# Running sums by token inside the expert loop, in place of a last stage that gathers the experts' rows

## The chip, the core and the metric

The kernel runs on one NeuronCore of a Trainium2 chip. The metric is the time of one execution in microseconds (us) on the device. Three executions of the kernel before took 1806.34, 1813.04 and 1813.47 us; the median is 1813.04 us. Engines: PE is TensorE (PEld its weight loads), ACT is ScalarE, DVE is VectorE, POOL is GpSimd, SP is SyncE, which here only issues transfers. Each engine runs its own instructions in order; a wait on a semaphore holds up everything behind it on that engine.

## The reference, cut to what matters

One layer of a streaming encoder for 1088 tokens (1024 of a prompt, 64 of a sample) of width 1024. The change touches its end:

```
  h = x + w_out( sum_b sigmoid(gate_b) * (o_b @ w_branch[b]) )
  h = h + HierMoE(rmsnorm(h))   (top-1 of 4 groups, then top-2 of 8 SwiGLU experts)
  y = rmsnorm_final(h)

def expert_block(args):
    xblk, e = args
    return (jax.nn.silu(xblk @ wg[e]) * (xblk @ wu[e])) @ wd[e]

def rmsnorm(x, g):
    x32 = x.astype(jnp.float32)
    y = x32 * lax.rsqrt(jnp.mean(x32 * x32, axis=-1, keepdims=True) + EPS)
    return (y * g.astype(jnp.float32)).astype(x.dtype)
```

Each token goes to 2 of the 32 experts, so there are 2176 pairs of token and expert, 68 for an expert in the mean. Each expert has three weight matrices of 2 MB. All is in float32.

## The kernel before

The program is a row of stages. The last one, which the change is in, is one block: gates and branches, the output projection (which leaves the rows h in SBUF as `mixT`, and `hlast` for the last 64 tokens), routing, 32 experts, and a tail.

**Routing** (VectorE `choose` and `take`, TensorE `count` and `enlist`) gives each pair a place: up to 128 tokens in the list of their expert. The list (`toks`) says which rows of the normalised h, kept in device memory as `ffn_rows` (`htd`), expert n needs. GpSimd fetches them by an indirect DMA into `xe` (L2021), two experts ahead at most.

**An expert** n on TensorE: `turn_x` transposes the fetched rows, `up(n,"g")` and `up(n,"u")` are the gate and up products, `turn_h` transposes the hidden rows, `down(n)` is the down product. In the order of the program `down(n-1)` comes after `up(n,"u")` and `turn_x(n+1)`, so one turn of the loop holds 72 matmuls of 512 columns. Each product is made in three passes from halves in a rounded format: of each half matrix (128x2048, 1 MB, six for an expert) ScalarE writes the high part `hig` (`split_high`, L2434), VectorE the low part `low`<-`raw`,`hig` (`split_low`, L2732). There are 8 buffers of raw and low halves and 6 of high ones. SP issues each 1 MB load as its buffer comes free.

**ScalarE's turn n** is written out by hand: two splits, `silu(n)` (L2496), `h_high(n-1)` (L2500), two splits, `x_high(n+1)` (L2489), two splits, `out(n-1)` (L2507), which copies the finished rows of expert n-1 from PSUM to `ye`, and the issue of their store to `expert_rows` (`ysd`, L2510). VectorE's turn has its six splits and `h_low`, `multiply`, `x_low`. In turns 8, 11 and 14 VectorE does, one a turn, `overflow`, `order` and `slots`, which work out the weights of the pairs and their places (`sidx`); `slots` ends with the semaphore `found`.

**The tail** begins when the experts' rows are in device memory. For nine tiles of tokens GpSimd gathers each token's two expert rows (`ya` L2033 and L2058, `yb` L2051); four tiles are summed on TensorE by diagonal matrices (L2318, L2327, L2334), five on VectorE (L2924, L2930). ScalarE squares and takes the root (L2577 to L2581), VectorE scales (L2937), SP stores.

A list of more than 128 tokens goes on in a loop of its own (`further`), which waits for `found` and does nothing for these inputs.

## Time and profile before

The profiled execution took 1812.19 us, of which the span from its first to its last instruction is 1810.5 us.

| engine | busy us | share of the span |
|---|---|---|
| PE | 1760.3 | 97% |
| DVE | 1047.7 | 58% |
| ACT | 860.7 | 48% |
| POOL | 118.8 | 7% |

The experts run from about 1192 us to 1763 us, a third of the span, with PE busy throughout; the tail is the rest. The 16 DMA engines are busy for all of the expert stage too. Shares over the whole span say little here: in the expert stage DVE is busy for nine tenths and ACT for eight tenths of the time, POOL for less than one.

### The profile page before, as it was taken

The page shows a single profiled execution, that of the slowest core. Times are in us where ns is not written, and L with a number is a line of the kernel's source. Part 1 is how long each engine was busy: PE and PEld are TensorE (multiplying, and loading weights), DVE is VectorE, ACT ScalarE, POOL GpSimd, SP SyncE. Part 2 cuts the span into 40 slices and gives each one's busy share as a digit, 9 for nine tenths or more (in the row PEclk, how much of TensorE's full clock was granted, in tenths as well). Part 3 has the DMA queues.
Part 4 walks back from the last instruction along what each step waited for, and adds up shares of the span by engine and source line. Part 5 has one row for each costly group of instructions (what it writes and reads, how often), then busy time and mean ns, then how long its engine had stood idle before and what let it go on. Part 6 is the DMA issues. An engine that isn't in the chain of part 4 may idle for free.

```text
span 1810.5 us, 25543 instructions
## 1 busy us (share of the span) xinstructions
PE 1760.3 (97%) x10346; PEld 1562.7 (86%) x10346; DVE 1047.7 (58%) x1303; ACT 860.7 (48%) x1093; POOL 118.8 (7%) x139
## 2 busy tenths in 40 slices
PE   8999999999999999999999999989999999999995
PEld 7888888988898899999999988878888888888872
DVE  5347775433445431223243255678989998898965
ACT  4225554331543331211122223268887878788863
POOL 0010000000000020000000000010000000000024
PEclk9999999999999999999999999989999999999997
DMA  5241111112122132222221232189999999999987
GB/s 189 85 120 30 31 32 37 35 32 60 35 64 83 41 98 64 88 63 83 70 99 47 76 146 71 65 331 403 419 408 417 414 413 415 414 415 415 415 290 262
DMA packets 140762, 329.42 MB, mean 182 GB/s; under 512 B 15978, under 2 KB 92646, under 8 KB 115941
## 3 DMA queue, kind: packets, MB, share of 16 engines
q1 hardware_dynamic: 123764, 272.25, 40.7%
q0 software_dynamic: 12128, 38.74, 5.9%
q10 hardware_dynamic: 4752, 16.78, 2.3%
q8 instruction: 84, 1.38, 0.3%
q14 instruction: 34, 0.28, 0.0%
HBM read 290.09 MB, written 39.87 MB: 182 GB/s over the span
## 4 chain that ended last, share of the span: by engine, by line
PE 61%; DVE 1%; DMA 1%; DVEq 0%; issue 0%; ACT 0%; ACTq 0%; POOLq 0%
PE banks L72 7%; PE banks L70 7%; PE banks L71 7%; PE banks L2233 6%; PE banks L2235 6%; PE banks L2234 6%; PE banks L2261 3%; PE banks L2259 3%; PE banks L2260 3%; PE banks L2112 2%; PE banks L2114 2%; PE banks L2113 2%; PE banks L2219 2%; PE banks L2243 1%; PE banks L2142 1%; DMA yb<-expert_rows,sidx 1%
## 5 line engine op out<-in xcount | busy, mean ns | idle before, releaser
L2732 DVE TENSOR_TENSOR low<-raw,hig 128x2048 fp32r<-128x2048 f32 x192 | 431.4, 2285 | 58.0 <-ACT hig L2434 55.6
L2434 ACT ACTIVATE hig<-raw 128x2048 fp32r<-128x2048 f32 x192 | 359.3, 1916 | 20.8 <-ACT ye L2507 14.5
L2233 PE MATMUL banks<-hig,xel 128*128 128x512 f32 x512 | 203.1, 397 | 0.2 <-DVE xel L2804 0.2
L2235 PE MATMUL banks<-hig,xeh 128*128 128x512 f32 x512 | 200.2, 391 | 0.0
L2234 PE MATMUL banks<-low,xeh 128*128 128x512 f32 x512 | 199.8, 390 | 0.0
L70 PE MATMUL banks<-xhi,glo 128*128 128x384 f32 (+1 forms) x552 | 180.0, 326 | 1.9 <-PEq L65 1.9
L72 PE MATMUL banks<-xhi,ghi 128*128 128x384 f32 (+1 forms) x552 | 180.0, 326 | 0.0
L71 PE MATMUL banks<-xlo,ghi 128*128 128x384 f32 (+1 forms) x552 | 179.9, 326 | 0.0
L70 PE MATMUL gproj<-xhi,glo 128*128 128x384 f32 (+1 forms) x384 | 130.1, 339 | 0.0
L72 PE MATMUL gproj<-xhi,ghi 128*128 128x384 f32 (+1 forms) x384 | 125.4, 326 | 0.0
L71 PE MATMUL gproj<-xlo,ghi 128*128 128x384 f32 (+1 forms) x384 | 125.2, 326 | 0.0
L2235 PEld LDWEIGHTS banks<-hig,xeh 128*128 128x128 f32 x512 | 96.4, 188 | 20.7
L2233 PEld LDWEIGHTS banks<-hig,xel 128*128 128x128 f32 x512 | 96.8, 189 | 19.6 <-DVE xel L2804 0.6
L2234 PEld LDWEIGHTS banks<-low,xeh 128*128 128x128 f32 x512 | 96.5, 189 | 19.0
L2625 DVE TENSOR_TENSOR tm<-sg,banks 128x384 f32<-128x384 f32 (+1 forms) x42 | 22.3, 532 | 152.2 <-PE banks L72 152.2
L836 DVE TENSOR_TENSOR_SCAN sfx<-sfx,over 128x896 f32<-128x896 f32 (+4 forms) x64 | 85.6, 1389 | 34.7 <-ACT sfx L672 34.7
L70 PEld LDWEIGHTS banks<-xhi,glo 128*128 128x128 f32 x552 | 103.6, 188 | 2.0 <-issue 2.0
L72 PEld LDWEIGHTS banks<-xhi,ghi 128*128 128x128 f32 x552 | 103.6, 188 | 0.0
L71 PEld LDWEIGHTS banks<-xlo,ghi 128*128 128x128 f32 x552 | 103.6, 188 | 0.0
L2259 PE MATMUL banks<-hig,htl 128*128 128x512 f32 x256 | 102.6, 401 | 0.0
L2261 PE MATMUL banks<-hig,hth 128*128 128x512 f32 x256 | 100.0, 391 | 0.0
L2260 PE MATMUL banks<-low,hth 128*128 128x512 f32 x256 | 99.9, 390 | 0.0
(484 smaller groups left out, 3510.9 us busy)
## 6 DMA issues: line engine op xcount, KB each, us to landing
raw<-in_w_e_gate_dram SPq DMA_DIRECT2D x64, 1024.0 KB, 8.1
raw<-in_w_e_up_dram SPq DMA_DIRECT2D x64, 1024.0 KB, 8.2
raw<-in_w_e_down_dram SPq DMA_DIRECT2D x64, 1024.0 KB, 7.5
graw<-in_w_in_dram SPq DMA_DIRECT2D x39, 512.0 KB, 3.8
expert_rows<-ye ACTq DMA_DIRECT2D x31, 512.0 KB, 8.3
xt<-in_x_prompt_dram SPq DMA_DIRECT2D x16, 512.0 KB, 3.6
expert_rows<-nil POOLq DMA_DIRECT2D x16, 512.0 KB, 4.0
braw<-in_w_branch_dram SPq DMA_DIRECT2D x24, 256.0 KB, 3.0
```

The costliest lines, as they stand in the source:

```text
L70: nc.tensor.matmul(out, wl, xh, start=(opens and i == 0), stop=False)
L71: nc.tensor.matmul(out, wh, xl, start=False, stop=False)
L72: last = nc.tensor.matmul(out, wh, xh, start=False, stop=(closes and i == len(parts) - 1))
L836: nc.vector.tensor_tensor_scan(v, v, cover, 1.0, ALU.mult, ALU.max).then_inc(scanned, 1)
L2233: nc.tensor.matmul(bank[:, :], xel[n % 2][:, kk, :], wh[:, k, :], start=(kk == 0), stop=False)
L2234: nc.tensor.matmul(bank[:, :], xeh[n % 2][:, kk, :], wl[:, k, :], start=False, stop=False)
L2235: last = nc.tensor.matmul(bank[:, :], xeh[n % 2][:, kk, :], wh[:, k, :], start=False, stop=(kk == KC - 1))
L2259: nc.tensor.matmul(bank[:, :], htl[n % 2][:, kk, :], wh[:, k, cols], start=(kk == 0), stop=False)
L2260: nc.tensor.matmul(bank[:, :], hth[n % 2][:, kk, :], wl[:, k, cols], start=False, stop=False)
L2261: last = nc.tensor.matmul(bank[:, :], hth[n % 2][:, kk, :], wh[:, k, cols], start=False, stop=(kk == 3))
L2434: nc.scalar.activation(hig[q % HI][:, :], raw[q % RAW][:, :], ACT.Copy).then_inc(high, 1)
L2732: nc.vector.tensor_tensor(low[q % RAW][:, :], raw[q % RAW][:, :], hig[q % HI][:, :].bitcast(F32), ALU.subtract).then_inc(lowed, 1)
```

## The change

The kernel after has no tail that gathers. A second array in device memory, `sum_rows` (`acd`), starts as a copy of h, a row for each token. Every expert adds its rows, already multiplied by the pair's weight, to the running sums. The lower-numbered expert of a token writes the sum back (`low_rows`); the higher-numbered one has the complete row of the token, so the final norm of that row is taken there and the row goes to the output (`out_rows`). Rows that a transfer shall leave out have an index beyond its bound.

- **GpSimd** for expert c: `sum_rows` (an indirect DMA that reads the token's sums and adds them into `ye`), two `out_rows` for expert c-2 (prompt and sample), `root_of(c-1)`: one multiplication of 128x1024 by the norm weight and 13 operations on one column with a drain behind each but the first (a root by Newton's steps), then the wait for `hr_in` and `low_rows`. `sum_rows` waits for `low_out`: the write-back of expert c-1 has to be in memory.
- **ScalarE**: `square(n-2)` after `silu(n)`, waiting for `hr_in`, that is for `sum_rows(n-2)`; and before `out(n-1)` a multiplication of a 128x1024 row block by the roots (waiting for `rooted_row`). The store is no longer issued here. For the first three experts GpSimd multiplies by the weight, since the weights by place are not there yet.
- **VectorE**: `overflow` and `order` at the end of turn 0, `slots` at the end of turn 1. `slots` now makes records of 8 words (`smeta`: token, weight, three destinations).
- **GpSimd before its loop**: 9 more stores (`sum_rows` from `mixT`), and after `found` 18 indirect scatters of the records by place, a wait for them, and two loads of the records in the experts' order (`meta`, 32 bytes for each place).
- The last two experts' sums are added on VectorE (`hr`), and the last three experts' rows are scaled there.

The diff, cut to its core:

```diff
+        def low_rows(pool, src, which, signal):
+            pool.indirect_dma_start(acd, bass.IndirectOffsetOnAxis(ap=which[:, 2:3], axis=0), src[:, :], None,
+                                    bounds_check=T - 1, oob_is_err=False).then_inc(signal, 16)
+
+        def out_rows(pool, src, which, signal):
+            pool.indirect_dma_start(yp, bass.IndirectOffsetOnAxis(ap=which[:, 3:4], axis=0), src[:, :], None,
+                                    bounds_check=FULL * P - 1, oob_is_err=False).then_inc(signal, 16)
+            pool.indirect_dma_start(ysm, bass.IndirectOffsetOnAxis(ap=which[:, 4:5], axis=0), src[:, :], None,
+                                    bounds_check=T - FULL * P - 1, oob_is_err=False).then_inc(signal, 16)
...
+            nc.gpsimd.tensor_scalar(tokg[:, :], tokf[:, :], float(-T), None, ALU.add)
+            nc.gpsimd.memset(smp[:, 0:FULL], float(FAR))
+            nc.gpsimd.tensor_scalar(smp[:, FULL:NT], tokf[:, FULL:NT], float(-FULL * P), None, ALU.add)
...
             for t in range(NT):
                 r = rows_of(t)
                 pool.wait_ge(ndone, t + 1)
                 pool.dma_start(htd[t * P:t * P + r, :], nrow[t % 2][0:r, :]).then_inc(kept[t % 2], 16)
+                pool.dma_start(wide(acd[t * P:t * P + r, :]), hrow(t, r)).then_inc(hkept, 16)
...
-            for n in range(NE):
+            def x_rows(n):
                 if n >= 2:
                     pool.wait_ge(xturned, 2 * n - 2)
+                places = toks2[:, n:n + 1] if n < 2 else toks[:, n:n + 1]
+                pool.indirect_dma_start(xe[n % 2][:, :], None, htd, bass.IndirectOffsetOnAxis(ap=places, axis=0),
+                                        bounds_check=T - 1, oob_is_err=False).then_inc(fetched[n % 2], 16)
+
+            def sum_rows(n, dst, compute):
+                pool.wait_ge(low_out, 16 * n)
+                pool.indirect_dma_start(dst[:, :], None, acd, bass.IndirectOffsetOnAxis(ap=toks[:, n:n + 1], axis=0),
+                                        bounds_check=T - 1, oob_is_err=False, compute_op=compute).then_inc(hr_in, 16)
+
+            def root_of(c):
+                pool.wait_ge(squared, c + 1)
+                ms, x, y, u = stat[:, c:c + 1], root[:, 0:1], root[:, 1:2], root[:, 2:3]
+                if c >= 2:
+                    pool.wait_ge(y_out[c % 2], 32 * (c // 2))
+                nc.gpsimd.tensor_tensor(yo[c % 2][:, :], ye[c % YE][:, :], gf[:, :], ALU.mult).then_inc(gained, 1)
+                nc.gpsimd.tensor_scalar(x, ms, EPS, None, ALU.add)
+                pool.drain()
+                nc.gpsimd.tensor_copy(u, x.bitcast(I32))
+                pool.drain()
+                nc.gpsimd.tensor_scalar(u, u, -0.5, 1597463007.0, ALU.mult, ALU.add)
+                pool.drain()
+                nc.gpsimd.tensor_copy(y.bitcast(I32), u)
+                pool.drain()
+                for _ in range(3):
+                    nc.gpsimd.tensor_scalar(u, y, y, x, ALU.mult, ALU.mult)
+                    pool.drain()
+                    nc.gpsimd.tensor_scalar(u, u, -0.5, 1.5, ALU.mult, ALU.add)
+                    pool.drain()
+                    nc.gpsimd.tensor_scalar(y, y, u, None, ALU.mult)
+                    pool.drain()
+                pool.wait_ge(gained, c + 1)
+                pool.sem_inc(rooted_row, 1)
+
+            def finish(c):
+                pool.wait_ge(scaled, c + 1)
+                out_rows(pool, yo[c % 2], meta[:, c, :], y_out[c % 2])
...
+            x_rows(2)
+            x_rows(3)
+            pool.wait_ge(filled, 16)
             pool.wait_ge(found, 1)
+            for t in range(NT):
+                for k in range(2):
+                    pool.indirect_dma_start(slot_meta, bass.IndirectOffsetOnAxis(ap=sidx[k][0:r, t:t + 1], axis=0),
+                                            smeta[0:r, t, k, :], None).then_inc(meta_out, 16)
+            pool.wait_ge(meta_out, 16 * 2 * NT)
...
+            for c in range(NE - 2):
+                if c + 4 < NE:
+                    x_rows(c + 4)
+                if c == 0:
+                    pool.wait_ge(meta_in0, 16)
+                if c == 4:
+                    pool.wait_ge(meta_in1, 16)
+                pool.wait_ge(emptied, c + 1)
+                if c < YE:
+                    nc.gpsimd.tensor_scalar(ye[c][:, :], ye[c][:, :], share(c), None, ALU.mult).then_inc(shared, 1)
+                    pool.wait_ge(shared, c + 1)
+                sum_rows(c, ye[c % YE], ALU.add)
+                if c >= 2:
+                    finish(c - 2)
+                if c:
+                    root_of(c - 1)
+                pool.wait_ge(hr_in, 16 * c + 16)
+                low_rows(pool, ye[c % YE], meta[:, c, :], low_out)
...
             def out(n):
-                if n >= 2:
-                    act.wait_ge(stored[n % 2], 16 * (n // 2))
+                if n >= YE:
+                    act.wait_ge(gained, n - YE + 1)
+                    act.wait_ge(low_out, 16 * (n - YE + 1))
                 act.wait_ge(used, place["d", n, 1] + 1)
+                if n == YE:
+                    act.wait_ge(meta_in0, 16)
+                if n == YE + 1:
+                    act.wait_ge(meta_in1, 16)
                 for half in range(2):
-                    last = nc.scalar.activation(ye[n % 2][:, half * 512:half * 512 + 512], [Z0, Z1][half][:, :], ACT.Copy)
+                    last = nc.scalar.activation(ye[n % YE][:, half * 512:half * 512 + 512], [Z0, Z1][half][:, :], ACT.Copy,
+                                                scale=share(n) if n >= YE else 1.0)
                 last.then_inc(emptied, 1)
+            def square(c):
+                if c < NE - 2:
+                    act.wait_ge(hr_in, 16 * c + 16)
+                else:
+                    act.wait_ge(joined, 1)
+                nc.scalar.activation(junk[:, :], ye[c % YE][:, :], ACT.Square, scale=D ** -0.5,
+                                     accum_out=stat[:, c:c + 1]).then_inc(squared, 1)
...
                     split_high(q0 + 4)
                     split_high(q0 + 5)
                     silu(n)
+                if 2 <= n < NE:
+                    square(n - 2)
...
                     split_high(q0 + 9)
                     if n == NE - 1:
                         h_high(n)
+                    if n >= 3:
+                        act.wait_ge(rooted_row, n - 2)
+                        nc.scalar.activation(yo[(n - 3) % 2][:, :], yo[(n - 3) % 2][:, :], ACT.Copy, scale=root[:, 1:2]).then_inc(scaled, 1)
                     out(n - 1)
...
+                nc.vector.memset(smf[:, :, :, :], 0.0)
...
+                both = lambda t: t[:, :].unsqueeze(2).to_broadcast([P, NT, 2])
+                nc.vector.tensor_copy(smf[:, :, :, 0], both(tokf))
+                nc.vector.tensor_tensor(smf[:, :, :, 2], pair[:, :, :], both(tokf), ALU.add)
+                ve.drain()
+                nc.vector.tensor_tensor(smf[:, :, :, 3], isov[:, :, :], both(tokf), ALU.add)
+                nc.vector.tensor_tensor(smf[:, :, :, 4], isov[:, :, :], both(smp), ALU.add)
...
+                nc.vector.tensor_copy(smeta[:, :, :, 1].bitcast(F32), wts[:, :, :]).then_inc(found, 1)
...
-                if n in (8, 11, 14):
-                    (overflow, order, slots)[(n - 8) // 3]()
+                if n == 0:
+                    overflow()
+                    ve.drain()
+                    order()
+                    ve.drain()
+                if n == 1:
+                    slots()
```

ScalarE in two turns of the expert loop. Before, from the end of one turn to the end of the next (`hig` is a split, `gl` the silu, `hth` h_high, `xeh` x_high, `ye` the rows of the finished expert):

```order
L2507 ACTIVATE ye_7119<-banks 128x512 x2
L2510 DMA expert_rows<-ye_7119 128x1024
L2434 ACTIVATE hig_7102<-raw_7084 128x2048
L2434 ACTIVATE hig_7103<-raw_7085 128x2048
L2496 ACTIVATE gl_7121<-banks 128x512
L2500 ACTIVATE hth_7112<-banks 128x512
L2434 ACTIVATE hig_7104<-raw_7086 128x2048
L2434 ACTIVATE hig_7105<-raw_7087 128x2048
L2489 ACTIVATE xeh_7108<-banks 128x512 x2
L2434 ACTIVATE hig_7100<-raw_7088 128x2048
L2434 ACTIVATE hig_7101<-raw_7089 128x2048
```

After, the same stretch up to the multiplication that now stands ahead of `ye`:

```order
L2525 ACTIVATE ye_7120<-banks,meta_7128 128x512 x2
L2448 ACTIVATE hig_7104<-raw_7086 128x2048
L2448 ACTIVATE hig_7105<-raw_7087 128x2048
L2509 ACTIVATE gl_7134<-banks 128x512
L2534 ACTIVATE junk_7127,stat_58<-ye_7120 128x1024
L2513 ACTIVATE hth_7114<-banks 128x512
L2448 ACTIVATE hig_7106<-raw_7088 128x2048
L2448 ACTIVATE hig_7107<-raw_7089 128x2048
L2502 ACTIVATE xeh_7110<-banks 128x512 x2
L2448 ACTIVATE hig_7102<-raw_7090 128x2048
L2448 ACTIVATE hig_7103<-raw_7091 128x2048
L2562 ACTIVATE yo_7124<-yo_7124,root_7071 128x1024
```

`junk,stat<-ye` is the square, which stands directly behind the silu and ahead of h_high and four splits; `yo<-yo,root` is the multiplication by the roots, with the next `ye` behind it; the store is gone.

GpSimd in the expert loop. Before, the last two of its 32 fetches, which stand one behind the other, and the first gathers of the tail:

```order
L2021 DMA xe_7106<-ffn_rows,toks_7116 128x1024
L2021 DMA xe_7107<-ffn_rows,toks_7116 128x1024
L2033 DMA ya_7130<-expert_rows,sidx_7041 128x1024
L2033 DMA ya_7138<-expert_rows,sidx_7041 64x1024
L2033 DMA ya_7131<-expert_rows,sidx_7041 128x1024
```

After, the last third of one expert's work and the first half of the next's (the column work on `root` stands 13 times for each expert):

```order
L2027 TENSOR_SCALAR root_7071<-root_7071 128x1
L2029 TENSOR_SCALAR root_7071<-root_7071 128x1
L2031 TENSOR_SCALAR root_7071<-root_7071 128x1
L1904 DMA sum_rows<-ye_7122,meta_7128 1088x1024
L2004 DMA xe_7109<-ffn_rows,toks_7118 128x1024
L2009 DMA ye_7120<-sum_rows,toks_7118 128x1024
L1908 DMA out_dram<-yo_7125,meta_7128 1024x1024
L1910 DMA out_dram<-yo_7125,meta_7128 64x1024
L2017 TENSOR_TENSOR yo_7124<-ye_7122,gf_7126 128x1024
L2018 TENSOR_SCALAR root_7071<-stat_58 128x1
L2020 CAST root_7071<-root_7071 128x1
L2022 TENSOR_SCALAR root_7071<-root_7071 128x1
```

The fetch of `xe` was all there was for an expert. Now the add from `sum_rows`, two stores to the output, the multiplication by `gf` and the chain on `root` stand between two write-backs to `sum_rows`.

## Rows read from the trace of the kernel before

**Rows 1.** Window in the expert stage: us, busy (count) by engine, PEclk, DMA share, GB/s.
```profile
1350.00:1400.00 50.00, 50.00 (x239) 41.97 (x238) 45.37 (x41) 40.85 (x36) 4.39 (x3) 1.00 1.01 413
```

**Rows 2.** Timeline of ACT, one turn: start, us, instruction, idle before it and its releaser.
```profile
1396.87 1.09 ACT L2489 ACTIVATE xeh<-banks 128x512 fp32r<-128x512 f32 x2 [1.29 <-PE banks L2219]
1397.84 3.72 ACT L2434 ACTIVATE hig<-raw 128x2048 fp32r<-128x2048 f32 x2
1402.85 1.09 ACT L2507 ACTIVATE ye<-banks 128x512 f32<-128x512 f32 x2 [1.28 <-PE banks L2261]
...
1404.40 3.72 ACT L2434 ACTIVATE hig<-raw 128x2048 fp32r<-128x2048 f32 x2 [0.47 <-ACT ye L2507]
...
1408.23 0.60 ACT L2496 ACTIVATE gl<-banks 128x512 f32<-128x512 f32 x1
1408.73 0.59 ACT L2500 ACTIVATE hth<-banks 128x512 fp32r<-128x512 f32 x1
...
1414.63 1.09 ACT L2489 ACTIVATE xeh<-banks 128x512 fp32r<-128x512 f32 x2 [1.70 <-PE banks L2219]
```

**Rows 3.** DMA issues, the end of a row being the median us to landing.
```profile
ffn_rows<-nrow POOLq DMA_DIRECT2D x1, 256.0 KB, 7.3
wr<-in_w_fine_dram POOLq DMA_DIRECT2D x4, 32.0 KB, 4.0
```

**Rows 4.** Tile xe: its 32 fetches, us from issue to landing.
```profile
DMA to landing us min/median/max: 4.4/8.6/9.8
```

**Rows 5.** Timeline, DVE's splits beside POOL's indirect DMAs, experts and last expert.
```profile
1411.79 4.49 DVE L2732 TENSOR_TENSOR low<-raw,hig 128x2048 fp32r<-128x2048 f32 x2
1415.30 1.80 POOL L2021 DMA_INDIRECT xe<-ffn_rows,toks  x1 [16.38 <-PE banks L2219]
1752.17 4.49 DVE L2732 TENSOR_TENSOR low<-raw,hig 128x2048 fp32r<-128x2048 f32 x2
1752.47 2.87 POOL L2033 DMA_INDIRECT ya<-expert_rows,sidx  x1 [0.30 <-issue]
```

**Rows 6.** Timeline about 130 us, and the group of DVE's line 789 (ns min/median/max).
```profile
129.85 1.68 POOL L361 TENSOR_TENSOR vn<-vsh,vn 64x512 f32<-64x512 f32 x1 [6.14 <-DMA vsh<-in_cache_sb_v_dram]
130.78 2.54 DVE L789 TENSOR_TENSOR vn<-vsh,vn 128x512 f32<-128x512 f32 x1
131.50 1.26 POOL L340 TENSOR_TENSOR cvs<-cvsh,cvs 128x512 f32<-128x512 f32 x1
...
L789 DVE TENSOR_TENSOR vn<-vsh,vn x8: 681/686/2535, 124.9 to 143.2; 128x512 f32<-128x512 f32 x8
```

**Rows 7.** POOL timeline, two casts with drains between; and a group of the tail.
```profile
3.36 0.59 POOL L345 CAST qbh<-nbias 64x64 fp32r<-64x64 f32 x2 [1.04 <-DVE identb L859]
...
L2051 POOL DMA_INDIRECT yb<-expert_rows,sidx x9 | 9.0, 997 | 4.2 <-issue 2.4 <-DMA expert_rows<-ye 1.8
```

**Rows 8.** ACT and DVE in turns 1 and 2; windows about `overflow`, `order` and `slots`.
```profile
1222.27 4.50 DVE L2732 TENSOR_TENSOR low<-raw,hig 128x2048 fp32r<-128x2048 f32 x2
1231.19 0.59 ACT L2500 ACTIVATE hth<-banks 128x512 fp32r<-128x512 f32 x1
...
1351.00:1353.00 2.00, 2.00 (x11) 1.65 (x10) 1.58 (x12) 1.85 (x2) 0.00 (x0) 1.00 0.97 365
1404.20:1406.90 2.70, 2.70 (x14) 2.23 (x13) 2.40 (x12) 2.50 (x2) 0.00 (x0) 1.00 1.03 413
1457.50:1461.70 4.20, 4.20 (x23) 3.54 (x21) 3.68 (x23) 3.93 (x3) 0.00 (x0) 1.00 0.99 394
```

**Rows 9.** The end: chain of waits (first two rows), then timeline of ACT and DVE.
```profile
1757.51 1.09 ACT ye L2507 x2
1765.83 9.93 DMA yb<-expert_rows,sidx
...
1797.18 1.04 ACT L2577 ACTIVATE junk<-ya 128x1024 f32<-128x1024 f32 x1
...
1798.51 1.28 DVE L2930 SCALAR_TENSOR_TENSOR ya<-ya,wts,yb 128x1024 f32<-128x1024 f32 x1
```

More of the change, by code:

```diff
@@ L2037, in body @@
+            c = NE - 2
+            sum_rows(c, hr, ALU.bypass)
+            finish(c - 2)
+            pool.wait_ge(joined, 1)
+            low_rows(pool, ye[c % YE], meta[:, c, :], low_out)
+            sum_rows(c + 1, hr, ALU.bypass)
+            for i in range(3):
+                c = NE - 3 + i
+                pool.wait_ge(last_scaled, i + 1)
+                out_rows(pool, last_yo[i], meta[:, c, :], y_out[c % 2])
             def body(b, e):
```

379 lines of the change are left out of this document (133 added, 246 removed).

## The prediction

> **What bounds the kernel now.** I read the windows first. In the expert stage PE has no gap: 50.00 of 50.00 us at a granted clock of 1.00, while DVE works 45.37, ACT 40.85 and POOL 4.39 us, and the DMA engines are busy throughout [rows 1]. The timeline of ACT shows the rhythm: x_high at 1396.87 and again at 1414.63, so an expert costs 17.76 us [rows 2]. Between, ACT idles only 3.4 us: 1.28 and 1.70 us waiting for PE, 0.47 us before it issues a store [rows 2]. So this stage goes at PE's pace, with ACT and DVE close behind. After the last matmul comes a tail: from the start of the copy of expert 30's rows (1757.51) to the end of the span (1810.5) it is 53.0 us, or 51.9 us from that copy's end, nearly all chain [rows 9]. The chain there shows one gather awaited for 9.93 us. The change trades this tail for work in a stage where ACT has 3.4 us an expert to spare, DVE some 1.6 us, and POOL, by its busy time, 16 us.
>
> The sum is made against the profiled execution: 1812.2 us, of which 1810.5 us are its span; that is 0.8 us under the median of 1813.04 us.
>
> **The tail: what goes and what comes.** From the end of the copy of expert 30's rows it now takes: an addition on DVE at 1.3 us; `low_rows(30)`; `sum_rows(31)`; two halves on DVE for expert 31, 1.3 us together; the second half of the square, 0.8 us with reading its sum; logarithm and exponential with drains, 0.7 us (estimate); scaling on DVE, 1.3 us; two stores, the second issued 1.3 us behind the first, and landed. The durations are those of L2930 (1.28) and half of L2577 (1.04) with its read-out [rows 9]; the issue is 1.0 us with 0.3 us behind it [rows 7]. Each round trip is priced at 4.4 us, the quickest fetch there was, since no weights are loaded then [rows 4]; at 8.6 us each it would be 12.6 us more. Sum: 1.3 + 4.4 + 4.4 + 1.3 + 0.8 + 0.7 + 1.3 + 1.3 + 4.4 = 19.9, with hops 20.9 us. Against 51.9 us that is **31 us gained**, between 18 and 34.
>
> **The start of the experts.** ScalarE's turn 2 has `square(0)` behind its silu, which waits for the sums of expert 0, and those need the records. Before, turn 2's h_high, right behind the silu, stood at 1231.19 [rows 8]. Now VectorE ends turn 1's splits at 1226.8; `overflow` (2.0 us), `order` (2.7 us) and `slots` (4.2 us, now about 5 as it has some more small steps) are put before `found` [rows 8]: 1226.8 + 2.0 + 2.7 + 5 = 1236.5. Then 18 scatters on POOL at 1.3 us [rows 7]: 1259.9. The last has to land, some 3.4 us after its issue (4.4 less 1.0) [rows 4, 7]; the first load of records takes 4 us, as one of 1024 pieces of 32 bytes does [rows 3]: 1267.3. A multiplication by the weight on POOL, 2 us (L340 takes 1.26 for two inputs of 512 columns [rows 6]), then `sum_rows(0)` at 7.3 us (priced below) and about 4 us because 3584 pieces of 32 bytes are ahead of it in its queue: 1280.6. So ACT stands from 1231 to about 1281. All that is behind it stands too: h_high(1), without which `down(1)` can't start, the splits for expert 3, x_high. PE runs out of work within 8 us. Nothing gives this back later, since PE has no slack: **50 us lost**; at best 35 (records in at once, fetch 4.4 us), at worst 85, if each of the 224 small pieces an engine has is served in turn with a 4 KB piece of weights. The nine extra stores of h during routing are beside idle DMA engines; I take 1 us for the last one, which is ahead of the first fetch, and count it in the hops.
>
> **Each expert, first by the round trip.** The add for expert c can be issued when `out(c)` is done. ACT then does two splits (3.7 us) and the silu, and comes to `square(c)` about 4.9 us after the end of `out(c)`: 1403.94 to 1408.83 [rows 2]. The transfer moves 68 rows or 272 KB in the mean. The nearest row is the 256 KB one that ran beside the first weight loads: 7.3 us; ends 4.4 and 9.8 us [rows 3, 4]. So ACT waits here in every turn. From the landing to the end of `out(c+1)` ACT has: square 1.2, h_high 0.5, two splits 3.6, x_high 1.0, two splits 3.6, the new multiplication 1.0, out 1.1 = 12.0 us [rows 2, 9]. The circle is 12.0 + 0.2 + 7.3 = 19.5 us against 17.76: 1.7 us more for each expert. It is free from 5.5 us down.
>
> **Then by POOL.** There is a second circle: `sum_rows(c)` must wait for the write-back of c-1, which POOL issues behind all its other work. From the issue of the add: 1.3; two stores 2.6; the multiplication of 1024 columns 2.5 (twice 1.26 [rows 6]); 13 column operations at 0.36 us, the spacing of two small casts with a drain between them (0.59 less 0.23 for one) [rows 7], 4.7; sum 11.1 us. `low_rows` then takes 6.5 us from issue to landing (136 KB: between 4.0 for 32 KB and 7.3 for 256 KB [rows 3]). That is 17.6 us, which would just fit into 17.76.
>
> But POOL does not run beside DVE's splits as if alone. At 1415.30 an indirect DMA was issued while the second of two splits ran until 1416.28; it took 1.80 us instead of 1.0 and ended 0.8 us after the split. At 1752.47 one ended 0.9 us after the first split of its pair (1754.42), 2.87 us in all [rows 5]. It goes the other way too: a VectorE subtraction that takes 686 ns took 2535 while POOL had two subtractions of its own until 132.76, and ended 0.56 us after them [rows 6]. Whoever is second waits for the other's instruction to end. The two-input splits, 2.24 us each and six for an expert, are 13.5 us of each turn. A chain of 13 dependent column operations that meets a pair of splits gets one operation through at each end of a split, in place of six.
>
> With these I lay out one turn from the issue of the add, with the landing at 7.3: splits of the down half run until about 3.6, those of the gate half from 11 to 15.5, those of the up half from 17.5. The two stores lose some 2.2 us to the first pair, the column chain, which would end at 13.3, loses 3.7 us to the second and ends at 17. The write-back lands at 17 + 6.5 = 23.5 us. **23.5 us for an expert**, 5.75 more than now. The low end is the round-trip circle at 4.4 us, which costs nothing; the high end is 27 us (write 8 us, four more waits of a split), 9.3 more. I take 5.75, since the lock is seen in rows on both sides. 28 turns (experts 1 to 29) see it: **161 us lost**.
>
> The Trainium skill says the same as a rule (SBUF — State Buffer, § Who interferes with whom): a VectorE instruction with two SBUF inputs contends with a GpSimd instruction that reads SBUF, as an exclusive lock held for the whole instruction. It would hold for the small column operations as well, which no row here shows; the trace agrees for indirect DMAs and for subtractions [rows 5, 6]. Without it the sum would be that of the round-trip circle.
>
> DVE gets less time too: POOL's multiplication by `gf` can block a split for 2.5 us, and DVE has 1.6 us to spare; in a turn of 23.5 us that is hidden.
>
> Sum: 1812.2 - 31 + 50 + 161 = **1992 us**.
>
> **Rivals.**
> *A, round trips only.* The small column operations slip by the splits, and ACT's wait for the add sets the pace at 19.5 us: 1812.2 - 31 + 50 + 28 x 1.7 = 1879 us. For it: only indirect DMAs and wide subtractions are seen to wait. Against it: column operations read SBUF through the same port as those.
> *B, latency hides.* With 68 rows in place of 128 the add lands within 5.5 us and POOL's chain fits. Then only start and tail count: 1812.2 - 31 + 50 = 1831 us. For it: fewer rows, and the fastest fetch at 4.4 us. Against it: the 256 KB transfer beside the weights took 7.3 us, and the median fetch took 8.6 [rows 3, 4]. The Trainium skill (DMA: Bandwidth & Descriptors, § Anatomy of one DMA — SWDGE path) puts a transfer at about 2.0 us plus its bytes at 436 GB/s, an estimate of 2.6 us for 272 KB, by which B would hold; for the 512 KB fetches it says 3.2 us and the trace 8.6, so I weigh it low.
> *C, the records come in time.* If ACT does not stand in turn 2 for longer than 31 us, and the turns stay at 17.76, the tail decides and the kernel is faster: at a stand of 15 us, 1812.2 - 31 + 15 = 1796 us. Against it: the 18 scatters alone are 23.4 us behind `found`, itself 5 us after ACT has arrived.
> *D, worse than laid out.* Turns at 27 us or over, or the small pieces at their dear price: 1812.2 - 31 + 50 + 28 x 9.3 = 2092 us and more.
>
> **How the numbers follow.** Forecast (turns of 21.5 to 26 us) 0.52, own range 1930 to 2070; A 0.25; B 0.08; C 0.04; D 0.11. The range for 8 in 10 leaves out C, most of B and most of D: 1845 to 2100 us. A change under 0.5% (9 us) can't be told from none. Faster by more holds only in C: 0.04. Within it: 0.02, from B with a shorter stand. Slower: 0.94.
>
> **What would show it.** In the changed profile: ACT idle for 40 to 60 us before `junk`<-`ye` in turn 2, PE idle with it; 18 `slot_meta`<-`smeta` scatters just before. Then x_high every 23 to 24 us (19.5 for A, 17.8 for B), POOL busy or held for most of a turn, and its `root` operations in clusters with gaps that end where a split of DVE ends. The add <-`sum_rows` landing at 6 to 8 us. The wait ahead of the add is for `low_out`, not for ACT's `ye`; if it is for ACT's `ye` in every turn, A holds. A span that ends about 21 us after the last expert but one is copied out shows the tail. The forecast fails if the column operations run at even spacing through the splits, or if the add lands within 5.5 us.

## The result

The changed kernel takes 2203.11 us (median of 4 executions, 2201.55 to 2207.49) where the kernel before takes 1813.16 us: a ratio of 1.2174, 95% interval 1.2154 to 1.2194. The profiled execution took 2201.55 us, its span 2199.9 us. The direction was forecast, the size was not: 390 us more in place of 180, outside the range of 1845 to 2100 us.

The span grew by 389.4 us. Three marks of the two timelines cut it up:

| stretch | before | after | difference |
|---|---|---|---|
| start of h_high(1), ScalarE's turn 2 | 1231.19 [rows 8] | 1272.00 | +40.8 |
| from there to the end of the copy of expert 30's rows | 527.4 us | 899.5 us | +372.1 |
| from there to the end of the span | 51.95 us | 28.47 us | -23.5 |

So nearly all of it is in the turns of the expert loop (the stretch holds 29 of them).

### The profile after

The window that answers to [rows 1], the same columns:

```profile
1400.00:1500.00 100.00, 69.49 (x289) 56.89 (x289) 54.24 (x36) 51.99 (x48) 62.85 (x62) 0.85 0.67 237
```

PE, without a gap before, is busy for 69 of 100 us. No engine is near its limit and the DMA engines are a third idle: this is a loop of waits, not a lack of throughput. The granted clock of PE is down to 0.85, a mean over stretches at the full clock (2.4 GHz) and at the lower one (1.2 GHz), but PE is waiting in any case.

One turn on GpSimd (start, length, engine, line, what; in brackets the idle time before):

```profile
1692.08 1.60 POOL L2009 DMA_INDIRECT ye<-sum_rows,toks  x1 [5.41 <-DMA sum_rows<-ye,meta]
1693.98 1.04 POOL L1908 DMA_INDIRECT out_dram<-yo,meta  x1 [0.30 <-issue]
1695.32 0.98 POOL L1910 DMA_INDIRECT out_dram<-yo,meta  x1 [0.30 <-issue]
1696.32 2.36 POOL L2017 TENSOR_TENSOR yo<-ye,gf 128x1024 f32<-128x1024 f32 x1
1698.76 0.24 POOL L2018 TENSOR_SCALAR root<-stat 128x1 f32<-128x1 f32 x1
1701.34 0.18 POOL L2020 CAST root<-root 128x1 f32<-128x1 int32 x1 [2.34 <-issue]
...
1703.23 2.41 POOL L2031 TENSOR_SCALAR root<-root 128x1 f32<-128x1 f32 x1 [0.17 <-issue]
1705.83 2.15 POOL L2027 TENSOR_SCALAR root<-root 128x1 f32<-128x1 f32 x1 [0.18 <-issue]
...
1709.74 2.06 POOL L2029 TENSOR_SCALAR root<-root 128x1 f32<-128x1 f32 x1 [0.16 <-issue]
1711.97 2.14 POOL L2031 TENSOR_SCALAR root<-root 128x1 f32<-128x1 f32 x1 [0.17 <-issue]
1715.07 1.06 POOL L1904 DMA_INDIRECT sum_rows<-ye,meta  x1 [0.96 <-issue]
1716.43 1.05 POOL L2004 DMA_INDIRECT xe<-ffn_rows,toks  x1 [0.30 <-issue]
1724.42 1.60 POOL L2009 DMA_INDIRECT ye<-sum_rows,toks  x1 [6.95 <-DMA sum_rows<-ye,meta]
```

The next add waits for the write-back (6.95 us), so GpSimd's circle sets the turn. (A drain stands behind each of the 13 column operations, the first too.) Two things in it are not as forecast. Ahead of the first cast, behind the first drain, there are 2.34 us that nothing named accounts for. And four operations on a single column take 2.1 to 2.4 us where their neighbours take 0.2 to 0.3. ScalarE and VectorE in that turn:

```profile
1699.80 1.06 ACT L2534 ACTIVATE junk<-ye 128x1024 f32<-128x1024 f32 x1 [9.97 <-DMA ye<-sum_rows,toks]
...
1701.34 3.70 ACT L2448 ACTIVATE hig<-raw 128x2048 fp32r<-128x2048 f32 x2
...
1714.25 1.15 ACT L2562 ACTIVATE yo<-yo,root 128x1024 f32<-128x1024 f32 x1 [4.64 <-POOLq L2034]
```

```profile
1701.47 0.69 DVE L2818 TENSOR_TENSOR htl<-banks,hth 128x512 fp32r<-128x512 f32 x1 [9.40 <-ACT hth L2513]
1703.27 4.49 DVE L2739 TENSOR_TENSOR low<-raw,hig 128x2048 fp32r<-128x2048 f32 x2 [1.11 <-ACT hig L2448]
...
1709.47 4.48 DVE L2739 TENSOR_TENSOR low<-raw,hig 128x2048 fp32r<-128x2048 f32 x2
```

The long column operations are those beside VectorE's splits. In the turn ahead of this one they are twice as long, one operation for both splits of a pair (GpSimd, then VectorE):

```profile
1672.60 4.57 POOL L2027 TENSOR_SCALAR root<-root 128x1 f32<-128x1 f32 x1 [0.18 <-issue]
...
1672.54 4.50 DVE L2739 TENSOR_TENSOR low<-raw,hig 128x2048 fp32r<-128x2048 f32 x2 [1.11 <-ACT hig L2448]
```

Between 1350 and 2100 us, 59 of the 312 operations on `root` are long, and each of the 59 ends 0.05 to 0.22 us after the end of a split: 34 take 2.0 to 2.5 us, 25 take 4.3 to 4.6 us. VectorE had stood idle for 9.40 us before, while ScalarE waited for the add; the landing of the add lets ScalarE, VectorE and GpSimd's chain go all at once. Averaged over 27 turns of the loop (worked out from the timelines):

| us from the issue of the add | forecast | measured |
|---|---|---|
| add landed, the square starts | 7.3 | 8.8 |
| second column operation starts | 8.6 | 10.1 |
| chain ends | 17.0 | 21.7 |
| write-back issued | 17.0 | 22.7 |
| next add issued (the turn) | 23.5 | 30.6 |

At the end, the last adds, writes and scaling run as described, in 28.5 us. The first row is expert 30's sum on VectorE, 6.2 us after the copy of its rows; the others are the last on GpSimd:

```profile
2177.64 1.23 DVE L2928 TENSOR_TENSOR ye<-ye,hr 128x1024 f32<-128x1024 f32 x1 [10.04 <-DMA hr<-sum_rows,toks]
...
2183.11 1.04 POOL L2009 DMA_INDIRECT hr<-sum_rows,toks  x1 [2.21 <-DMA sum_rows<-ye,meta]
...
2188.34 0.96 POOL L1910 DMA_INDIRECT out_dram<-yo,meta  x1 [0.30 <-issue]
2192.36 0.96 POOL L1908 DMA_INDIRECT out_dram<-last_yo,meta  x1 [3.06 <-DVE last_yo L2934]
2193.62 0.96 POOL L1910 DMA_INDIRECT out_dram<-last_yo,meta  x1 [0.30 <-issue]
```

### The profile page after: what moved, and what is told of

Read it like the earlier page. It is cut to its first block and busy times, and to the rows that moved or that the text cites. A ratio compares the mean times of both kernels' runs of the same rounds, so it can differ in the third digit from the quotient of the medians.

```text
span 2199.9 us, 26544 instructions
## 1 busy us (share of the span) xinstructions
PE 1806.6 (82%) x10298; PEld 1600.5 (73%) x10298; DVE 1033.9 (47%) x1280; ACT 907.0 (41%) x1154; POOL 641.1 (29%) x666
## 5 line engine op out<-in xcount | busy, mean ns | idle before, releaser
L2302 PE MATMUL banks<-hig,htl 128*128 128x512 f32 x256 | 132.2, 516 | 343.4 <-DVE htl L2818 343.4
L2302 PEld LDWEIGHTS banks<-hig,htl 128*128 128x128 f32 x256 | 64.6, 252 | 364.3 <-DVE htl L2818 349.4
L2534 ACT ACTIVATE junk<-ye 128x1024 f32<-128x1024 f32 x31 | 32.7, 1056 | 373.3 <-DMA ye<-sum_rows,toks 367.8
L2818 DVE TENSOR_TENSOR htl<-banks,hth 128x512 fp32r<-128x512 f32 x32 | 22.1, 691 | 343.9 <-ACT hth L2513 343.7
L2303 PE MATMUL banks<-low,hth 128*128 128x512 f32 x256 | 125.0, 488 | 0.0
L2304 PE MATMUL banks<-hig,hth 128*128 128x512 f32 x256 | 122.0, 477 | 0.0
L2031 POOL TENSOR_SCALAR root<-root 128x1 f32<-128x1 f32 x87 | 107.1, 1231 | 14.8 <-issue 14.8
L2278 PEld LDWEIGHTS banks<-hig,xeh 128*128 128x128 f32 x512 | 96.2, 188 | 20.6
```

What stands on the lines that cost most here:

```text
L2031: nc.gpsimd.tensor_scalar(y, y, u, None, ALU.mult)
L2278: last = nc.tensor.matmul(bank[:, :], xeh[n % 2][:, kk, :], wh[:, k, :], start=False, stop=(kk == KC - 1))
L2302: nc.tensor.matmul(bank[:, :], htl[n % 2][:, kk, :], wh[:, k, cols], start=(kk == 0), stop=False)
L2303: nc.tensor.matmul(bank[:, :], hth[n % 2][:, kk, :], wl[:, k, cols], start=False, stop=False)
L2304: last = nc.tensor.matmul(bank[:, :], hth[n % 2][:, kk, :], wh[:, k, cols], start=False, stop=(kk == 3))
```

## The experiments

The theory after the first look: (a) a drain on GpSimd also waits for every transfer that GpSimd has under way, so the chain can't start before the add and the stores have landed; (b) that start coincides with VectorE's splits, which hold up the chain. The rivals: the forecast's A (ScalarE's wait for the add sets the turn), and that the slow column operations or the gap have some other cause. All kernels start from the changed one (2203 us). The turn, and its parts, are means in us over 27 or 28 turns. "Add landed" counts from the add's issue; "chain" is the time from the second column operation's start to the last one's end.

| run | us | turn | add landed | chain | what differs |
|---|---|---|---|---|---|
| changed kernel | 2203 | 30.6 | 8.8 | 11.6 | |
| e1 | 2025 | 24.0 | 11.2 | 4.0 | semaphores for drains |
| e2 | 2089 | 26.8 | 11.4 | 2.5 | no Newton steps (leaves out part of the root) |
| e3 | 2200 | 30.7 | 10.0 | 10.5 | write-back ahead of the chain |
| e4 | 2192 | 30.1 | 10.2 | 10.1 | e1 and e3 |
| e5 | 2089 | 26.8 | 7.3 | 5.9 | square at the end of the turn |
| e6 | 2183 | 30.2 | 10.1 | 10.0 | splits of VectorE halved |
| e7 | 2063 | 25.9 | 7.6 | 5.9 | e1 and e5 |
| e8 | 2149 | 28.4 | 15.2 | 4.0 | e1 and e6 |
| e9 | 1972 | 22.7 | 9.8 | - | root on VectorE, two Newton steps |
| e10 | 1934 | 21.6 | 11.6 | - | e9, square late, write-back first |
| e11 | 2215 | 31.0 | 11.1 | 9.0 | stores behind the write-back |
| e12 | 1907 | 20.6 | 10.5 | - | e10, fetch behind the add |

### e1: semaphores in place of drains

```
+            def link(inst):
+                inst.then_inc(linked, 1)
+                links[0] += 1
+                pool.wait_ge(linked, links[0])
...
-                nc.gpsimd.tensor_copy(u, x.bitcast(I32))
-                pool.drain()
+                link(nc.gpsimd.tensor_copy(u, x.bitcast(I32)))
```

> GpSimd's 13 column operations are tied together by a semaphore each in place of a drain; nothing else. The changed kernel has a mean turn of 30.6 us. Theory (the turn is one chain on GpSimd: the add lands 8.8 us after its issue, a drain that waits for every transfer GpSimd has under way ends 1.3 us later, 12 column operations held up by VectorE's splits take 11.6, the write-back is issued 1.0 later and lands after 8.0): without drains the chain starts some 7 us after the add's issue in place of 10.1, so 3 us less for each expert, 2203 - 28 x 3 = about 2120 us, and the idle time ahead of the first cast falls from 3.1 us a turn to 0.2. Rival (that idle time is VectorE's lock or a fixed cost of the chain): 2203 us, within 10.

Measured: 2024.62 us, 178 us less, twice what was expected (some 83). One turn on GpSimd, first and last rows of the chain:

```profile
1706.62 2.83 POOL L2009 DMA_INDIRECT ye<-sum_rows,toks  x1 [6.11 <-ACT ye L2525]
...
1713.25 2.40 POOL L2024 TENSOR_TENSOR yo<-ye,gf 128x1024 f32<-128x1024 f32 x1
1715.75 0.24 POOL L2025 TENSOR_SCALAR root<-stat 128x1 f32<-128x1 f32 x1
1716.05 0.18 POOL L2026 CAST root<-root 128x1 f32<-128x1 int32 x1
...
1719.79 0.28 POOL L2032 TENSOR_SCALAR root<-root 128x1 f32<-128x1 f32 x1
1720.99 2.78 POOL L1904 DMA_INDIRECT sum_rows<-ye,meta  x1 [0.92 <-POOL root L2032]
```

The gap ahead of the cast is gone, and every column operation is short. VectorE's timeline says why:

```profile
1703.50 8.89 DVE L2739 TENSOR_TENSOR low<-raw,hig 128x2048 fp32r<-128x2048 f32 x4
1718.74 0.69 DVE L2818 TENSOR_TENSOR htl<-banks,hth 128x512 fp32r<-128x512 f32 x1 [6.35 <-ACT hth L2513]
1720.54 4.50 DVE L2739 TENSOR_TENSOR low<-raw,hig 128x2048 fp32r<-128x2048 f32 x2 [1.11 <-ACT hig L2448]
```

The chain (1715.75 to 1720.07) now lies between VectorE's splits, while VectorE waits for the add as everyone does. So the drain cost twice: 3.0 us of waiting ahead of the first cast, and a chain longer by 7.6 us, nearly all of it because the chain was pushed from that free place into the splits. (Where no split is near, two operations follow each other every 0.34 us with a semaphore and every 0.41 us with a drain, which makes 0.8 us of it.) The turn shrank by 6.6 us and not by both, since another wait takes over: the next add now waits for ScalarE's copy (142.8 us in 25 waits, 5.7 each), no longer for the write-back. What is left is rival A's circle with a slower add than it assumed: 11.2 us to land and 12.8 from there to the next issue, 24.0 us.

### e11 and e2: which transfer the drain waits for

e11 puts the two stores behind the write-back (with a wait for ScalarE's multiplication ahead of the chain, which overwrites the root).

```
                 sum_rows(c, ye[c % YE], ALU.add)
-                if c >= 2:
-                    finish(c - 2)
                 if c:
                     root_of(c - 1)
                 pool.wait_ge(hr_in, 16 * c + 16)
                 low_rows(pool, ye[c % YE], meta[:, c, :], low_out)
+                if c >= 2:
+                    finish(c - 2)
```

> Drains and chain kept as in the changed kernel; only the two stores to the output stand behind the write-back in place of behind the add. Theory (a drain waits for all of GpSimd's transfers under way, the last of them being a store, which lands 1.3 us after the add): the first cast then starts at the landing of the add, 1.3 us earlier, and the add itself has less beside it: 28 x 1.5 us less, 2160 us (2130 to 2180), and the idle time ahead of the first cast ends within 0.4 us of the square's start on ScalarE. Rival (the drain waits for the add alone or for something else): 2203 us and a gap that still ends over 1 us behind the square's start.

The mechanism came out as stated, the time did not. In the changed kernel the cast starts 1.33 us after the square in the mean; here 0.30 us (median 0.31). But the stores now stand in GpSimd's queue ahead of the next add, which lands 2.3 us later (11.1 against 8.8): 2214.7 us, where 2160 was expected.

e2 is the same from the other side:

```
-                for _ in range(3):
+                for _ in range(0):
```

> Leaves out the three Newton steps (9 of the 13 column operations for an expert), so the roots are rough. Theory (the chain on GpSimd is the turn, its operations each wait for a split of VectorE now and then): 9 operations at a mean of 1.02 us and 0.17 us between them go, 10.7 us for each expert, but the turn then meets ScalarE's circle (12.0 us from landing to the next copy, and the add's 8.8) at 20.8 us: 2203 - 28 x 9.8 = about 1930 us. Rival A (the transfers' round trips and ScalarE's wait for the add set the turn, the chain lies beside them): above 2170 us. Rival B (the operations cost 0.36 us each, as unlocked): 28 x 3.2 us less, 2113 us.

This kernel leaves out the refinement, so its roots are rough; it is here for its times alone. 2089.15 us, 114 less in place of 270. Both the theory's number and rival A's are missed; rival B's is nearest, by accident: the operations that went saved 9.0 us of chain a turn, and the drain's wait grew by 4.5. One turn:

```profile
1812.96 0.98 POOL L1910 DMA_INDIRECT out_dram<-yo,meta  x1 [0.30 <-issue]
1813.95 2.41 POOL L2017 TENSOR_TENSOR yo<-ye,gf 128x1024 f32<-128x1024 f32 x1
1816.45 0.23 POOL L2018 TENSOR_SCALAR root<-stat 128x1 f32<-128x1 f32 x1
1824.73 1.08 POOL L2020 CAST root<-root 128x1 f32<-128x1 int32 x1 [8.05 <-issue]
```

The drain held for 8.05 us. The add had landed at 1819.98; the last store, issued at 1812.96, landed at 1824.40, and the cast starts 0.33 us later. The stores land later here (11.1 us after their issue in the mean, 6.3 in the changed kernel), and the drain passes it on. That they do so because a shorter turn crowds the transfers is likely, not shown: the DMA engines are busy for 0.95 of the time that an add is under way, 0.78 in the changed kernel.

The same can be read in every turn. From the last landing of an add or a store ahead of it to the cast it is 0.29 to 0.63 us in all 27 turns of the changed kernel, 0.29 to 0.33 in e2 and 0.25 to 0.33 in e11, whichever transfer is the last. Without drains (e1) the cast comes 7.1 us before that landing in the mean. This settles (a).

### e3 and e4: the write-back ahead of the chain

```
                 if c >= 2:
                     finish(c - 2)
+                pool.wait_ge(hr_in, 16 * c + 16)
+                low_rows(pool, ye[c % YE], meta[:, c, :], low_out)
                 if c:
                     root_of(c - 1)
-                pool.wait_ge(hr_in, 16 * c + 16)
-                low_rows(pool, ye[c % YE], meta[:, c, :], low_out)
```

> The write-back of expert c is issued as soon as its add has landed, ahead of the multiplication and the column chain for c-1; drains kept. Theory (a drain waits for GpSimd's transfers under way): the chain can't start before the write-back has landed, so the same parts stand in another order, 8.8 + 8.0 + 1.3 + 11.6, and the multiplication (2.4 us) is hidden: about 30 us a turn, 2160 to 2220 us. Rival (drains wait for nothing but GpSimd's own operations): the write-back's landing is hidden by the chain, the turn is 8.8 + 2.4 + 11.6 + 1 = 24 us, 2203 - 28 x 6.6 = 2018 us.

> Both edits: the write-back ahead of the chain, and semaphores in place of the drains. Theory: now the chain does run while the write-back lands: 8.8 + 1.1 + 2.4 + 11.6 = 24 us a turn, 2203 - 28 x 6.6 = about 2018 us, although the first edit alone gave some 84 us and the second next to nothing. Rival (drains are not what waits): the same time as the run that only moves the write-back.

e3 gave 2200.49 us, the time expected, but not for the reason: the DMA engines are busy for only 0.14 of the time that the write-back is under way there, it lands 2.8 us after its issue (median), under the multiplication, and no drain had to wait for it. e4 gave 2192.49 us, not 2018, so close to e3 that its rival, by which drains are not what waits, would have called it right. Its chain, without a single drain:

```profile
1702.55 2.16 POOL L2025 TENSOR_SCALAR root<-stat 128x1 f32<-128x1 f32 x1
1704.78 2.09 POOL L2026 CAST root<-root 128x1 f32<-128x1 int32 x1
1706.95 0.20 POOL L2027 TENSOR_SCALAR root<-root 128x1 f32<-128x1 f32 x1
...
1708.62 4.53 POOL L2030 TENSOR_SCALAR root<-root 128x1 f32<-128x1 f32 x1
```

Here it is the wait for the add, ahead of the write-back, that lets the chain start only when VectorE's splits start, and the chain takes 10.1 us again. The operations of e1 and e4 are the same; only their place against the landing differs, and that is 4.0 against 10.1 us. With the 59 ends above, this shows (b). The turn then closes over ScalarE: root, multiplication by it, copy, next add (ScalarE waits 7.0 us a turn for the roots).

### e6 and e8: shorter splits

```
-                nc.vector.tensor_tensor(low[q % RAW][:, :], raw[q % RAW][:, :], hig[q % HI][:, :].bitcast(F32),
-                                        ALU.subtract).then_inc(lowed, 1)
+                for cols in (slice(0, 1024), slice(1024, 2048)):
+                    last = nc.vector.tensor_tensor(low[q % RAW][:, cols], raw[q % RAW][:, cols],
+                                                   hig[q % HI][:, cols].bitcast(F32), ALU.subtract)
+                last.then_inc(lowed, 1)
```

> VectorE's subtraction of 2048 columns is two of 1024; nothing else of the changed kernel. Theory (a column operation of GpSimd waits for the end of the running split): each wait is half as long, 12 operations take 4.0 us unhindered (as in the run without drains) and 11.6 now, so 3.8 us less for each expert: about 2095 us, and no column operation takes more than some 1.3 us where the longest was 2.4 (or 4.5 for two splits). Rival (the long column operations have another cause): 2203 us and the same lengths.

> Semaphores in place of drains, and VectorE's subtractions halved. Theory: the chain already runs unhindered (4.0 us), so the 3.8 us a turn that halving is expected to bring to the kernel with drains are not there; only the issue of the add (2.8 us beside a split) gets shorter by 1 us a turn: 1990 to 2025 us. Rival (halving helps by making VectorE or the splits faster, not by the waits of the chain): the same gain as in the kernel with drains, 106 us, 1920 us.

e6: 2182.65 us. The chain is shorter by 1.6 us a turn, not 3.8. Some waits halved (50 column operations take 1.0 to 1.4 us), others still last for two or three halves (36 of 2.1 to 2.3 us, six up to 3.47 us); and the add landed 1.3 us later. e8 was a miss the other way: 2149.38 us, 125 slower than e1. The chain stayed at 4.0 us, as (b) has it, but the issue of the add did not get shorter:

```profile
1720.44 7.64 POOL L2009 DMA_INDIRECT ye<-sum_rows,toks  x1 [8.95 <-ACT ye L2525]
```

```profile
1717.45 9.16 DVE L2740 TENSOR_TENSOR low<-raw,hig 128x1024 fp32r<-128x1024 f32 x8
```

It took 7.64 us (also the median), began beside the third of eight halves without a gap and ended 1.5 us after the last. Beside four whole splits, in e1, the same issue took 2.83 us: it began beside the second and ended 1.5 us after that one's end, beside the third. So a wait is not simply the rest of the instruction under way: GpSimd can be passed over at the boundary between two instructions, as it was by the operations of 4.3 to 4.6 us of the changed kernel. What decides who comes next stays open.

### e5 and e7: the square at the end of ScalarE's turn

```
-                if 2 <= n < NE:
-                    square(n - 2)
...
+                    if n >= 2:
+                        square(n - 2)
                     if n >= 3:
                         act.wait_ge(rooted_row, n - 2)
```

> Drains kept; ScalarE's square of expert n-2 stands at the end of turn n, ahead of the multiplication by the roots, in place of behind the silu, so that h_high and four splits no longer wait for the add to land. Theory (GpSimd's circle of add, drain, chain, write-back sets the turn, and the chain now meets splits of VectorE at any place of the turn): 28 to 30 us a turn, the stand at the start shorter by 11 us, about 2150 us (2110 to 2190). Rival A of the prediction (ScalarE's wait for the add sets the turn): it would fall to 19 or 20 us, 1890 to 1910 us.

> Semaphores in place of drains and the square at the end of the turn. In the run with semaphores alone (2025 us) the column chain took 4.0 us, since it ran while ScalarE and so VectorE stood waiting for the add, and the turn was 24.0 us = 11.2 for the add + 12.8 on ScalarE. Theory (it is the standstill of VectorE that frees the chain): without the standstill the chain meets splits again, 9.4 + 8.5 + 1 + 6 = 25 us a turn: 1980 to 2070 us, so nothing gained or little. Rival (ScalarE's circle was all that was left, the chain stays at 4 us): 9.4 + 4 + 1 + 4 = 18.4 us a turn, 1870 us.

e5: 2088.5 us, 22 under the low end of what was expected, and far from rival A. e7: 2062.76 us, inside what was expected, and 38 us slower than e1: to take ScalarE's wait for the add away costs time there. In both ScalarE now waits for the roots in its place (10.4 us a turn in e5, 228.4 us in 22 waits), the chain meets the splits it happens to meet (5.9 us) and GpSimd's circle sets the turn. e7's time came out by parts that offset each other, the chain 2.6 us cheaper, its start 1.8 us later and the write-back 1.9 us dearer than laid out. That the chain came out at 5.9 and not 8.5 us was not foreseen: while ScalarE waits for the chain, VectorE runs dry, and the rest of the chain meets no split.

### e9, e10, e12: what is left without the chain

```
                 if c:
-                    root_of(c - 1)
+                    gain_of(c - 1)
...
                     h_low(n - 1)
+                if 3 <= n < NE:
+                    root_of(n - 3)
```

That is e9: `gain_of` is the multiplication by `gf` alone, and `root_of` now stands in VectorE's turn, with two Newton steps in place of three. e10 has the square late as in e5, and on GpSimd the order add, multiplication, write-back, stores. e12 changes one thing more:

```
             for c in range(NE - 2):
-                if c + 4 < NE:
-                    x_rows(c + 4)
...
                 sum_rows(c, ye[c % YE], ALU.add)
+                if c + 4 < NE:
+                    x_rows(c + 4)
```

> GpSimd's column chain and its drains are gone; VectorE takes the root (10 column operations, two Newton steps, once an expert, behind h_low). GpSimd keeps the multiplication by gf. Theory: as in the run with semaphores the turn is ScalarE's circle, 11.2 us for the add to land after its issue and 12.8 from there to the next issue, since the chain on GpSimd lay beside it: 2010 to 2040 us. Rival (GpSimd's time is what still bounds the run with semaphores): 5 us a turn less, 1885 us.

> The root on VectorE, the square at the end of ScalarE's turn, and on GpSimd the order add, multiplication, write-back, stores. Theory: no circle is left but add and write-back (7.7 us to land, 0.3, 7 to land: 15 us), less than PE's 17.76 us, and what is left over is VectorE's own time: 16.1 us a turn, 2.2 for the root, 2.4 for GpSimd's multiplication: 20.5 us a turn, 2203 - 28 x 10.1 - 11 at the start = about 1910 us (1860 to 1960). Rival (with PE at full speed the transfers take longer, so that add and write-back bind again): 22 us a turn and more, 1950 us or above. Rival B of the prediction (everything hides): 1831 us.

> As the last version but the best (root on VectorE, square late, write-back ahead of the stores), with one change: the fetch of xe for expert c+4 is issued behind the add of expert c in place of ahead of it. That version has a mean turn of 21.6 us, 12.45 from the add's issue to the write-back's and 9.1 from there to the next add. Theory (two serialised round trips are what is left, and the fetch ahead of the add in GpSimd's queue delays the add): the add lands 2 us sooner, of which the write-back, now behind the fetch, gives one back: 28 us less, 1905 us (1885 to 1920). Rival (the queue's order doesn't matter, the transfers wait for the weights' transfers beside them): 1934 us, within 10. Neither beats the kernel before (1811 us): at 17.76 us a turn two round trips would have to fit in, and they take 20.

e9: 1972.01 us, below the theory's 2010 to 2040 and far from its rival's 1885: the turn is still ScalarE's circle (the add waits for the copy of `ye` in 23 turns, 8.9 us each), but with GpSimd idle the add lands after 9.8 us, not 11.2. e10: 1934.0 us, inside what the theory gave but not for its reason. Add and write-back, put at 15 us together, took 11.6 and 7.7 us to land and with the steps between them fill the turn of 21.6 us, as the rival had it. e12: 1907.1 us (4 executions, 1905.16 to 1908.78; 1.0534 of the kernel before, 1.0515 to 1.0553), as expected, with parts about half of those laid out: the add lands 1.1 us sooner, the rest of the turn is 0.2 us longer. e12's window, and its two longest waits on GpSimd:

```profile
1400.00:1500.00 100.00, 93.13 (x437) 76.76 (x436) 90.25 (x100) 77.86 (x73) 57.01 (x29) 1.00 0.97 359
```

```profile
POOL ye L2009 <- DMA sum_rows<-ye,meta: 81.1, 20, 6.1
POOL sum_rows L1904 <- DMA ye<-sum_rows,toks: 76.6, 23, 5.9
```

What is left is two round trips in a row, 11.3 us for the add and 9.3 for the write-back with what is queued about it, 20.6 us a turn, and PE and VectorE at nine tenths. e12 is the best of the twelve and does not beat the kernel before: 28 turns at 2.9 us over 17.76 are 80 of its 95 us.

## Why the prediction was wrong

- **The tail.** Forecast 31 us gained (18 to 34), measured 23.5, inside the bounds. It is 28.5 us long where 20.9 was laid out. The sum began with VectorE's addition, as if expert 30's sums were there when its rows are; they were fetched only then, and the addition started 6.2 us later. The last 4.0 us, from the landing of the last store to the end of the span, stood in no term; the write-back landed quicker than its 4.4 us.
- **The start.** Forecast 50 us lost, measured 40.8. As described: 18 scatters, 1.4 us apart from 1230.81 on, the multiplication by the weight from 1260.72, the square at 1270.95 after 43.91 us of waiting. `found` came 5.7 us sooner than laid out, and the first add landed 6.5 us after its issue, not 11.3: the small pieces ahead of it (2.1 us to land) cost it nothing that shows. ScalarE's h_high(1) would have stood 3 us earlier than before without the stall. That the tail's miss (7.5 us) and the start's (9.2 us) nearly cancel is luck.

```profile
1230.81 2.23 POOL L2057 DMA_INDIRECT slot_meta<-smeta,sidx  x1 [31.44 <-DVE smeta L2894]
...
1254.59 0.90 POOL L2057 DMA_INDIRECT slot_meta<-smeta,sidx  x1 [0.30 <-issue]
1256.86 2.43 POOL L2061 DMA_DIRECT2D meta<-slot_meta  x2 [1.37 <-DMA slot_meta<-smeta,sidx]
...
1264.40 1.71 POOL L2009 DMA_INDIRECT ye<-sum_rows,toks  x1 [0.79 <-POOL ye L2072]
```

- **Each expert: the step that failed.** The circle was named rightly: the next add waits for the write-back. What failed is the term for the chain. "13 column operations at 0.36 us, the spacing of two small casts with a drain between them" priced a drain with nothing under way [rows 7], and the layout let the chain run on from the multiplication, so that it met only one pair of splits. It put nothing for the drain's wait for GpSimd's transfers, which is 3.0 us a turn. Of the 7.1 us a turn that were missing, 1.5 are the later start of the chain (10.1 against 8.6 us; the first column operation is done at 7.1), 3.2 its greater length, 1.0 the last drain and wait ahead of the write-back, and 1.5 what follows: the write-back lands after 7.1 us, not 6.5, and the next add is issued 0.8 us behind it. The first two are one cause: the drain ties the chain to the landing, and the landing starts the splits. e1 prices this cause at 178 us, of which the semaphores' shorter links can be some 20, out of the 211 us by which the loop was forecast too short. The count of turns was off as well: 29 of them lie between the marks, not 28, one turn's excess of 13 us.
- **The lock** was real. A pair of splits held the chain for some 4 us, near the 3.7 laid out; what was off is how many pairs it met. In 18 of 27 turns it met two, and those turns take 32.1 us in the mean; with one pair they take 27.7. That one operation gets through at the end of each split was wrong in 25 of 59 waits, which lasted for both splits (4.57 us above). The Trainium skill (SBUF — State Buffer, § Who interferes with whom) calls it an exclusive lock that blocks whoever comes second for the whole instruction. The trace agrees, for operations on one column too (2.41 us in place of 0.28); that the block ends with that instruction it does not bear out: 4.3 to 4.6 us in the changed kernel, 7.64 in e8.
- **Rival A** was the right circle for what comes behind the chain, at another price: the add lands after 11.2 us in e1, not 7.3.
- **Rival B** fell: between 1350 and 1900 us the quickest add of the changed kernel landed after 6.8 us. The Trainium skill's figures (DMA: Bandwidth & Descriptors, § Anatomy of one DMA — SWDGE path) make an estimate of 2.6 us for 272 KB, 2.3 for the 136 KB of a write-back. The trace comes near it only with little beside the transfer. The write-back takes 2.8 us in e3, where the DMA engines are busy for 0.14 of its time, and 7.1 in the changed kernel, where they are busy for 0.98 of it.

## What to carry to other kernels

Read what an instruction waits for against what is under way when it is reached in the new place, not against its price in a quiet part of the program. In a loop where several engines wait for the same landing, they all start at once: ask what they share. A transfer that has to come back within each turn costs its full latency under load, here 7 to 12 us for the add and some 7 to 8 us for the write-back beside the weights, and two of them in a row were more than the turn had.

## What the runs showed of the hardware

- A drain on GpSimd waits until the transfers that GpSimd has under way have landed: in the changed kernel the operation behind it starts 0.35 us after the last landing in the mean (27 turns), in e11 0.33 and in e2 0.33. A semaphore from the instruction itself doesn't wait for them: in e1 that operation starts 7.1 us before the last landing.
- An indirect DMA that adds takes GpSimd 1.60 us to issue alone, one that only reads 1.04 (`hr`<-`sum_rows`).
- A GpSimd operation on one column is held by a VectorE subtraction with both inputs in SBUF until 0.05 to 0.22 us after the end of it (59 of 59), or of the next one (25 of these).
- Beside back-to-back instructions of VectorE an issue on GpSimd can be held through several of them: 7.64 us, from the third to the last of eight.
- The latency of one and the same transfer goes with how busy the DMA engines are beside it: the write-back lands after 2.8 us at a DMA share of 0.14 (e3), 7.1 us at 0.98.
- With PE idle for a third of the time its granted clock was 0.85 in the window above, 1.00 in e12's.
